# An mLSTM stage with its exponents summed on TensorE in f32r, its read-out packed into three PSUM banks, and two reloads set beside compute

## The reference, in what matters

```python
dmat = jnp.where(_lower_tri(l), fc_t[..., :, None] - fc_t[..., None, :] + ig_t[..., None, :], -jnp.inf)
m_t = jnp.maximum(m_inter, jnp.max(dmat, axis=-1))
wmat = jnp.einsum('bclhk,bcshk->bhcls', q, k) * jnp.exp(dmat - m_t[..., None])
num = wmat @ v + s_inter * (q @ c_st)          # c_st: the state before the chunk
den = sum(wmat) + s_inter * (q @ n_st)
h = num / jnp.maximum(jnp.abs(den), floor)[..., None]
...
hm = jax.nn.sigmoid(o_pre) * hm                # then a norm per head, and the output projection
```

## Time and profile before

| | |
|---|---|
| median of three executions | 2985.6 us |
| the profiled execution, its own time | 2990.29 us |
| its span in the trace | 2988.1 us |
| the stretch that the change touches | 437.7 to 641.0 us of the span |

### The profile page before, as it was taken

The page is one execution under the profiler, slowest core; times in us unless marked ns, Lnnn a source line. Parts: engine busy times, 40 slices in busy tenths (PEclk is TensorE's granted clock), DMA queues, the critical chain, the costliest instruction groups (busy, mean ns, idle before and its releaser), DMA issues. The chain is left out here.

```text
span 2988.1 us, 30861 instructions
## 1 busy us (share of the span) xinstructions
PE 2602.6 (87%) x10919; PEld 1948.5 (65%) x10919; DVE 1433.0 (48%) x2228; ACT 967.6 (32%) x1621; POOL 286.5 (10%) x286
## 2 busy tenths in 40 slices
PE   5999987748999898998899897897959788599996
PEld 4777765537788785766788786774846667344442
DVE  4766536644555434634555534178982554311112
ACT  3422420133544335423544323333323423011111
POOL 0000001010000000000000002342520150001011
PEclk9999997769999998999999998997975699699998
DMA  3222320041333321202233312230210021599997
GB/s 132 69 101 81 106 69 1 10 173 29 99 98 84 128 100 58 85 29 99 71 98 96 117 68 99 77 113 25 89 57 1 22 85 38 227 353 369 369 365 255
DMA packets 214728, 339.18 MB, mean 114 GB/s; under 512 B 13877, under 2 KB 110013, under 8 KB 214493
## 3 DMA queue, kind: packets, MB, share of 16 engines
q1 hardware_dynamic: 208861, 316.79, 30.8%
q0 software_dynamic: 5760, 20.97, 1.9%
HBM read 304.18 MB, written 33.55 MB: 113 GB/s over the span
## 5 line engine op out<-in xcount | busy, mean ns | idle before, releaser
L366 PE MATMUL ps<-ffn_h_hi,ffn_w_hi 128*128 128x512 f32 x704 | 275.6, 392 | 10.9 <-DVE ffn_h_lo L361 10.9
L367 PE MATMUL ps<-ffn_h_lo,ffn_w_hi 128*128 128x512 f32 x704 | 275.3, 391 | 0.0
L368 PE MATMUL ps<-ffn_h_hi,ffn_w_lo 128*128 128x512 f32 x704 | 275.2, 391 | 0.0
L366 PE MATMUL ps<-wo_hi,lhs_hi 128*128 128x512 f32 x608 | 242.4, 399 | 33.7 <-DVE lhs_lo L361 33.7
L367 PE MATMUL ps<-wo_lo,lhs_hi 128*128 128x512 f32 x608 | 241.0, 396 | 0.0
L368 PE MATMUL ps<-wo_hi,lhs_lo 128*128 128x512 f32 x608 | 240.9, 396 | 0.0
L3802 PE MATMUL ps<-ring,expert_x 128*128 128x512 f32 x512 | 229.2, 601 | 8.7 <-issue 5.9
L361 POOL TENSOR_TENSOR w_lo<-ring,w_hi 128x512 fp32r<-128x512 f32 (+1 forms) x112 | 154.3, 1379 | 758.9 <-ACT w_hi L518 758.4
L3802 PEld LDWEIGHTS ps<-ring,expert_x 128*128 128x128 f32 x512 | 98.5, 193 | 133.7 <-issue 130.3
L361 DVE TENSOR_TENSOR wo_lo<-ring,wo_hi 128x1024 fp32r<-128x1024 f32 x76 | 93.0, 1224 | 185.5 <-ACT wo_hi L653 185.5
L2201 DVE SCALAR_TENSOR_TENSOR y_tmp<-ps,pcol,y_tmp 128x511 f32<-128x511 f32 x88 | 61.9, 746 | 219.9 <-ACT y_tmp L2173 219.9
(11 more groups left out here) (582 smaller groups left out, 5327.6 us busy)
## 6 DMA issues: line engine op xcount, KB each, us to landing
ring<-in_w_up SPq DMA_DIRECT2D x32, 2048.0 KB, 11.7
ring<-in_ffn_w_up SPq DMA_DIRECT2D x88, 512.0 KB, 4.9
moe_down<-in_w_down SPq DMA_DIRECT2D x32, 1024.0 KB, 9.7
ring<-in_ab_w_in SPq DMA_DIRECT2D x13, 2048.0 KB, 7.9
ring<-in_w_in SPq DMA_DIRECT2D x11, 2048.0 KB, 7.8
ring<-in_ffn_w_down SPq DMA_DIRECT2D x10, 2048.0 KB, 7.8
expert_results<-expert_y SPq DMA_DIRECT2D x32, 512.0 KB, 9.9
ring<-in_c_w_in SPq DMA_DIRECT2D x6, 2048.0 KB, 9.0
```

The source lines that it names most:

```text
L366: nc.tensor.matmul(out, left[0], right[0], start=start, stop=False, **more)
L367: nc.tensor.matmul(out, left[0], right[1], start=False, stop=False, **more)
L368: return nc.tensor.matmul(out, left[1], right[0], start=False, stop=stop, **more)
```

## The change

In words, ahead of the diff's core:

- `mlstm_mix`: the exponent is summed in PSUM by three f32r matmuls: the one-hot column with the high and the low part of `nm`, and a 128x128 tile `barred` (0 inside the triangle, -1e30 outside it) with four identities side by side. ScalarE takes its Exp straight from PSUM, with `u` as the bias, in four instructions a unit. VectorE multiplies it with the scores from PSUM. The cut at 0 and the masked copies of the scores go. `si` is spread by two f32r matmuls. Both kinds of row have two banks, and `rows` runs two units ahead, issued behind `mix` and `scores`. The eight 128x129 results of a head lie three, three and two to a bank; the read-out is two absolute values, a maximum, a reciprocal, two products with a broadcast factor, and one sum. Chunks with a zero state lose their second product.
- `mlstm_states`: only six states are kept. The zeroing goes, and the first step of each direction writes its state without the GpSimd product and the sum. ScalarE and VectorE split `nm` and `si` into two f32r parts here; VectorE makes `barred` and the four identities. SyncE loads o here, and ScalarE takes its Sigmoid here.
- The first chunk of the output weights is loaded during `mlstm_mix`; x and the second chunk are loaded during `gated_norm`. The block at L2065 goes. `project_out` waits for x before it adds it.

```diff
 def mlstm_states(k, r, k_cm, v, cst, kw, o, o_dram):
+        @block.sync
+        def _(sp):
+            for t in range(NT):
+                sp.dma_start(o[:, t, :], o_dram[t * P:(t + 1) * P, :]).then_inc(k.param_loaded.sem, 16)
...
-            nc.gpsimd.memset(cst[:, 0, 0, :, :], 0.0)
-            nc.gpsimd.memset(cst[:, 1, NT - 1, :, :], 0.0)
+            for n, (d, c) in enumerate(steps[2:], 2):
+                pool.wait_ge(*k.vc(n - 1))
+                nc.gpsimd.tensor_tensor(state_of(cst, d, c + 1 - 2 * d), state_of(cst, d, c), per_head(r.sold[:, d, c, :]), ALU.mult).then_inc(k.ga.sem, 1)
+        @block.scalar
+        def _(act):
+            nc.scalar.copy(r.nm_hi[:, :, :], r.nm[:, :, :]).then_inc(k.sa.sem, 1)
+            nc.scalar.copy(r.si_hi[:, :, :], r.si[:, :, :]).then_inc(k.sa.sem, 1)
+            act.wait_ge(*k.param_loaded(16 * NT))
+            for t in range(NT):
+                nc.scalar.activation(o[:, t, :], o[:, t, :], ACT.Sigmoid)
...
             weigh(0)
+            dve.wait_ge(*k.sa(1))
+            rest(nc.vector, r.nm_lo[:, :, :], r.nm[:, :, :], r.nm_hi[:, :, :])
+            for d in DIRS:
+                nc.vector.tensor_scalar(r.barred[:, d, :], k.tri[1 - d][:, :], -1.0, BIG, ALU.add, ALU.mult)
+            nc.vector.tensor_copy(r.ident4[:, :].rearrange(...), spread(k.ident[:, :]..., [P, NT, P]))
             for n, (d, c) in enumerate(steps):
                 if n + 1 < len(steps):
                     weigh(n + 1)
+                if n == 1:
+                    dve.wait_ge(*k.sa(2))
+                    rest(nc.vector, r.si_lo[:, :, :], r.si[:, :, :], r.si_hi[:, :, :])
                 dve.wait_ge(*k.pb(n + 1))
+                if n < 2:
+                    nc.vector.tensor_tensor(nxt, banks(), per_head(r.sloc[:, d, c, :]), ALU.mult).then_inc(k.vb.sem, 1)
...
+                    continue
 def mlstm_mix(k, g, r, q_cm, k_cm, v, cst, hm, b, first_out):
+        @block.sync
+        def _(sp):
+            load_weights(k, sp, first_out)
             def rows(n):
...
+                pick = spread(r.ident4[0:H, h:h + 1], [H, P])
+                if n >= 2:
+                    pe.wait_ge(*k.sa(n - 1))
+                at = k.ps[:, ARG + n % 2, :]
+                nc.tensor.matmul(at, pick, r.nm_hi[:, d, :], start=True, stop=False)
+                nc.tensor.matmul(at, pick, r.nm_lo[:, d, :], start=False, stop=False)
+                nc.tensor.matmul(at, r.barred[:, d, :], r.ident4[:, :], start=False, stop=True).then_inc(k.pa.sem, 1)
+                if n >= 2:
+                    pe.wait_ge(*k.va(n - 1))
+                nc.tensor.matmul(k.ps[:, SI[n % 2], :], pick, r.si_hi[:, d, :], start=True, stop=False)
+                nc.tensor.matmul(k.ps[:, SI[n % 2], :], pick, r.si_lo[:, d, :], start=False, stop=True).then_inc(k.vd.sem, 1)
             def mix(n):
...
+                if d == 0 and h >= 1:
+                    pe.wait_ge(*k.da(h))
...
             scores(0)
             rows(0)
+            rows(1)
+            for n, (h, d) in enumerate(units):
+                mix(n)
+                if d == 1 and h + 1 < H:
+                    scores(h + 1)
+                if n + 2 < len(units):
+                    rows(n + 2)
+            def weights(n):                                   # ScalarE
...
+                for c in range(NT):
+                    last = nc.scalar.activation(b.e[:, n % 2, tok(c)], k.ps[:, ARG + n % 2, tok(c)], ACT.Exp, bias=g.u[:, d, c, h:h + 1])
         @block.vector
...
             def prepare(n):
...
+                nc.vector.tensor_tensor(b.qs[:, n % 2, :], q_cm[:, h, :], k.ps[:, SI[n % 2], :], ALU.mult).then_inc(k.va.sem, 1)
+                dve.wait_ge(*k.pc(h + 1))
                 dve.wait_ge(*k.sa(n + 1))
+                nc.vector.tensor_tensor(b.w[:, n % 2, :], b.e[:, n % 2, :], k.ps[:, S, :], ALU.mult).then_inc(k.vb.sem, 1)
             def read_out(h):
...
+                nc.vector.tensor_tensor(b.parts[:, 0:6, :]..., k.ps[:, NUM:NUM + 2, 0:3 * MW]..., spread(r.rden[:, 0:6]..., [P, 2, 3, ML_D]), ALU.mult)
+                nc.vector.tensor_tensor(b.parts[:, 6:8, :], k.ps[:, NUM + 2, 0:2 * MW]..., spread(r.rden[:, 6:8]..., [P, 2, ML_D]), ALU.mult).then_inc(k.da.sem, 1)
                 dve.drain()
+                nc.vector.tensor_tensor(hm[:, :, h * ML_D:(h + 1) * ML_D], b.parts[:, 0:NT, :], b.parts[:, NT:2 * NT, :], ALU.add)
...
+            gated_norm(k, k.ytmp, o, ML_H, k.pcol[:, 0, 112:120], hm_cm, work, True, after=[x_again, wo[1]])
         project_out(..., scratch=work, x_back=k.x_back)
```

More of the change, by code:

```diff
@@ L718, in project_out @@
     k.param_loaded.close(32 if gain is not None else 16)
+    if x_back is not None:
+        x_back.close(16)
     if gain is not None:
@@ L1733, in mlstm_mix, with tok, carries @@
     units = [(h, d) for h in range(H) for d in DIRS]
-    arg, gg, w, qs, qk = (buf[:, n, :, :] for n in range(5))
-    NUM, SUMS, SI, QK = 0, 4, 5, 6
+    NUM, S, SI, ARG = 0, 3, (4, 7), 5
     def num(c, d):
-        return k.ps[:, NUM + c, d * 256:d * 256 + MW]
+        n = d * NT + c
+        return k.ps[:, NUM + n // 3, (n % 3) * MW:(n % 3 + 1) * MW]
+    def tok(c):
+        return slice(c * P, (c + 1) * P)
+    def carries(c, d):
+        return c != (0 if d == 0 else NT - 1)
     with nc.Block(no_gpsimd_drain=True) as block:
+        @block.sync
+        def _(sp):
+            load_weights(k, sp, first_out)
         @block.tensor
@@ L1794, in prepare @@
[L1794 to L1799, removed]
+                dve.wait_ge(*k.vd(n + 1))
                 if n >= 2:
                     dve.wait_ge(*k.pb(n - 1))
-                nc.vector.tensor_tensor(qs[:, d, :], q_cm[:, h, :], k.ps[:, SI, :], ALU.mult).then_inc(k.vd.sem, 1)
@@ L1820, in read_out @@
+                nc.vector.tensor_tensor(b.parts[:, 6:8, :], k.ps[:, NUM + 2, 0:2 * MW].rearrange("p (e w) -> p e w", w=MW)[:, :, 0:ML_D],
+                                        spread(r.rden[:, 6:8].rearrange("p (e o) -> p e o", o=1), [P, 2, ML_D]), ALU.mult).then_inc(k.da.sem, 1)
                 dve.drain()
-                for c in range(NT):
-                    last = nc.vector.scalar_tensor_tensor(out=hm[:, c, at], in0=num(c, 1)[:, 0:ML_D], scalar=r.rden[:, c, 1:2], in1=hm[:, c, at],
-                                                          op0=ALU.mult, op1=ALU.add)
@@ L1852, in mlstm_mix @@
         s.close(n)
-    for s in (k.pc, k.vc, k.da, k.sb):
+    for s in (k.pc, k.da, k.sb):
         s.close(H)
@@ L1872, in _ @@
             for w in after:
-                load_weights(k, sp, w)
+                if callable(w):
+                    w(sp)
+                else:
+                    load_weights(k, sp, w)
         @block.gpsimd
```

177 lines of the change are left out of this document (73 added, 104 removed).

## The result

The changed kernel takes 2947.9 us (median of four executions, 2934.9 to 2958.3) against 2987.8 for the kernel before on the same chip: a ratio of 0.986, 95% interval 0.9836 to 0.9884. It is faster, but by 40 us and not by the 61 that the sum gave, and 2947.9 lies above the range of 2915 to 2941. The profiled execution has a span of 2948.5 (before: 2988.1).

A forecast was written before the change was run, and what follows sets the result against it. Bounds by stretch: VectorE in the states, a TensorE-VectorE chain with falling clock in the mix, then a wait for data. -24.2 + 0.2 - 36.8 = -60.8 us, on the median's footing 2925; range 2915 to 2941.

The forecast's parts named there:

- Part 1: Reloads between mix and gated norm: moving the loads removes the whole hole, -24.2 us; bounds -24.2 and -22.
- Part 2: States: VectorE loses two sums, gains the rests of nm and si and small passes; +0.2 us, bounds -1 and +3.
- Part 3: Mix: falls from 112.9 to 76.1 us, -36.8; bounds -40.5 and -4.5.
- Which clock?: Mix: TensorE's pause becomes about 1.2 us, so only a few per cent of low clock; 8.7 us a head.
- the price of the rows: Mix: one spread of rows, five f32r matmuls of 512 columns, costs 1.35 us at 2.4 GHz.
- the head of 8.4: Mix: the chain of one head at 2.4 GHz, summed to 8.33 us, 8.4 with hand-overs.
- the change of kind: Mix: switching between kinds of matmul adds 0.2 us to a spread of rows.
- Rows 8 and 9: Profile rows of the last block: a TensorE pause of 1.38 us left the clock at 0.99 over 16 us.
- A: Rival for the mix: clock behaves as before, half the time at 1.2 GHz; mix -27, 2935 us; chance 0.16.
- B: Rival for the mix: clock stays at 1.2 GHz, only -4.5 us there, 2957 us; chance 0.05.
- D: Rival for mix: K=8 f32r matmuls cost 1.0 us each, clock low half the time; slower, 3006 us; chance 0.03.
- C: Rival at gated norm and projection: a transfer stays visible, returning at most 8 us; 2933 us; chance 0.04.

The follow-up runs named there:

- the kernel with the new order: The changed kernel, with only the rows of the second next unit issued ahead of a head's first products; 2928.3 us, ratio 0.9797.

## Why the prediction was wrong, by its steps

**The forecast as a whole.** The direction and parts 1 and 2 were right. In part 3 the step "Which clock?" failed and took the number out of the range, and the price of the rows was too low. By the traces the mix is 19.3 us longer than the sum had it, the rest behind it 4.3 longer, the states 0.5 longer, and they start 2.7 earlier (not isolated by a run).

**Part 1, right.** The hole is gone whole; o landed 7.7 us into the states (459.14), its Sigmoid ended at 463.0, before the states' 478.9. x and the second chunk cost nothing beside the norm (22.22 against 22.20), and the projection does not wait for them (67.8 us from its start to the next stage's first load, 67.6 in before). Both table loads, at 453.41 and 479.21, lie beside other engines' work, as taken. The batching rule of the Trainium skill (ScalarE: Activation LUTs, Table sets: the hidden batching unit) had no price here.

**Part 2, right within its bounds.** 27.5 against 26.8: +0.7 for a +0.2. The rest of nm took 1.20 as taken, that of si 1.76.

**Part 3, VectorE and ScalarE right.** The read-out is 0.96 and 0.41 us, the four Exps of a unit take 1.14 (reckoned: 1.13), and no weights wait for an Exp.

**Part 3, the rows' price, too low.** I took 1.35 us a unit from f32r matmuls of 128 partitions and named that gap ("no row shows one with K=8"). It was 1.73. With 0.38 more the head of 8.4 becomes 8.78, and 8.79 was measured at 2.4 GHz. At height 128 the same five take 1.23, and in a run of matmuls of 8 partitions they are 0.23 apart too. So the 0.23 of rows 6 was right for either height, and the 0.2 for the change of kind was too small: a unit has four changes of height, and together they came to about 0.5.

**Part 3, which clock: the failed step.** I argued from the length of pauses, and took 8.7 us a head and 17 for the first. The premise that the pause alone decides was false. Rows 8 and 9 were read for their pause; that their matmuls contract over 128 partitions stood in the same line (128*128), as 8*128 did at 512.90 in the earlier trace rows. The runs put in its place: with rows of 8 partitions the clock is 0.50 with TensorE busy for 14.00 of 14.00 us, and it falls without a pause in the kernel with the new order; with rows of 128 it is 1.00 across a pause of 1.42 to 1.45 in every head. The mix goes from 95.3 to 68.6 us by the height alone. The pause itself was reckoned too long (1.2; measured 0.51 to 0.85), so even the premise would have spoken for a high clock. The fall at 516 that I read in the earlier trace rows coincides with a pause, but also follows two row matmuls; the kernel before with rows of 128 shows that both count there, since there pauses of 2.22 and 2.57 us cost it in two of six heads instead of in every one. The Trainium skill (TensorE: Matmul & The Clock Gate, What's actually happening) ties the clock to how busy TensorE has recently been. The trace agrees in that an idle stretch is followed by 1.2 GHz (3.0 us idle at the start of the mix with full height, then 0.55 in its first 6.6 us), and disagrees where busy stretches stay there; the measurements decide, and busy time alone is not what counts. How the activity is counted, no run shows.

**The terms of the mix.** The sum counts a head from one read-out's end to the next. So counted, the first takes 21.8 us (479.2 to the first product of the second head, 500.99) instead of 17, the six between 66.9 instead of 52.2, and the last 6.7 (567.92 to 574.6) against 6.9. The first head stayed at 1.2 GHz to its maximum and still went 2.0 over the 19.8 named for that case, mostly because a unit's rows took 2.9 to 3.0 us at 1.2 GHz where 2.35 was taken. The 6.9 is written down too high; its terms add up to 6.6.

**The rivals.** The result lies between A's 2935 and B's 2957, and the sign that the prediction gave for them came: heads above 10 us with PEclk below 0.8. What they say of the clock holds in part: it was low in the first head and in three of six middle ones. Neither has the reason; A counts on the pause. I gave B 0.05 with the argument that the clock "rose again in less than that" before; in that trace it rose at 508 and at 522, behind eight products and within the scores, all of 128 partitions. D is refuted: rows were 0.31 to 0.44 apart, not 1.0. Its own sum has an error besides: with its mix of 42 + 6 heads the kernel is slower than before from 15.8 us a head on, not from 18.5. C is refuted by the norm's 22.22 and the projection's 67.8. In the second trace of the changed kernel only two of the middle heads ran at 1.2 GHz (mix 89.7), and that execution took 2944.8, with 2351.5 for the remainder behind the projection's start: still above the range.

## What to carry to other kernels

Read the contraction height in the trace's tile sizes (8*128, 64*128) beside the granted clock. Where TensorE is busy without a gap for long and the clock is still 0.50, look for matmuls over few partitions, and pad one operand with zeros up to 128. It costs a memset and one tile (and two copies for the keys, 2.2 us with the memsets), and it makes those matmuls no slower here. It gave 22 us in the mix (2944.9 to 2922.6) and, in an attention, 38 to 51. A pause's length alone is no argument about the clock until the matmuls on both sides of it are of full height; then 1.4 us kept it here and 2.2 us did not always.

## What the runs showed of the hardware

- With matmuls over 8 to 64 partitions among those of 128, the clock was 1.2 GHz for long stretches in which TensorE was hardly or never idle, in two unrelated stages, in f32 and in f32r (14.00 of 14.00 us busy at 0.50 in the mix, 83.61 of 84.30 at 0.50 in the attention). The same products padded with zeros ran at 0.94 to 1.00 over the mix and at 0.97 in the attention, so zeros in the added rows were enough. It is no fixed rule: heads with rows of 8 also ran at 1.00.
- Heights of 32 and 64 gave 0.84 in the mix, 8 gave 0.71 to 0.78; 64 in the attention gave 0.50.
- A matmul of 512 columns takes 0.23 us from start to start at 2.4 GHz at 8 partitions as at 128, between others of its height. Next to a change of height it takes 0.32 to 0.44.
- Of one kernel's executions, heads at 1.2 GHz come in different numbers (mix 95.3 and 89.7 us in two traces of the changed kernel), and its time goes from 2934.9 to 2958.3 us.
